# Seven block products for the second half of the output gate, with the queues around them reordered

## What is computed

```python
mod = c_act @ w_ada[l] + b_ada[l]
shift, scale, gate = jnp.split(mod, 3, axis=-1)
h = rms_norm_2(x, norm_g[l]) * (1.0 + scale[:, None, :]) + shift[:, None, :]
u = h @ w_in[l]
rg_x, rg_z, ml_x, ml_o, ml_z = jnp.split(u, split_pts, axis=-1)   # 1024 columns each
y_rg = rglru(causal_depthwise_conv(rg_x, ...), ...) * jax.nn.silu(rg_z)
y_ml = mlstm_branch(ml_x, ml_o, ...) * jax.nn.silu(ml_z)
y = jnp.concatenate([y_rg, y_ml], axis=-1) @ w_out[l]
x = x + gate[:, None, :] * y
...
# in mlstm_branch:
q = block_diag(xc, w_q); k = block_diag(xc, w_k); v = block_diag(xm, w_v)
gates = jnp.concatenate([q, k, v], axis=-1) @ w_if + b_if     # 8 columns: the "gate rows"
h = jax.nn.sigmoid(heads(o_pre)) * cell                       # o_pre is ml_o: the "output gate"
```

## Time and profile before

| | |
|---|---|
| median of 3 runs | 949.74 us (949.29 to 950.51) |
| the profiled execution's own time | 950.09 us |
| its span, first to last instruction | 948.4 us |
| TensorE busy | 877.4 us (93%) |
| DVE busy | 555.6 us (59%) |
| ACT busy | 252.9 us (27%) |
| POOL busy | 97.6 us (10%) |

### The profile page before, as it was taken

The page is one execution under the profiler, slowest core; times in us unless marked ns, Lnnn a source line. Parts: engine busy times, 40 slices in busy tenths (PEclk is TensorE's granted clock), DMA queues, the critical chain, the costliest instruction groups (busy, mean ns, idle before and its releaser), DMA issues.

```text
span 948.4 us, 14585 instructions
## 1 busy us (share of the span) xinstructions
PE 877.4 (93%) x5710; PEld 712.0 (75%) x5710; DVE 555.6 (59%) x1086; ACT 252.9 (27%) x550; POOL 97.6 (10%) x103
## 2 busy tenths in 40 slices
PE   8999999999999977766899999998999999999896
PEld 7878887888555544332789987997878898889785
DVE  4278857646222222103586893978657689667793
ACT  2356333013112110012144152032122703412311
POOL 5156000021000000001000000050000000006011
PEclk9999999999999998889899999999999999999999
DMA  9939885898999999999452633222544433522221
GB/s 342 409 140 347 363 322 209 333 422 350 367 423 420 419 420 421 421 422 384 82 208 98 223 149 119 93 86 89 187 168 168 166 134 140 216 89 90 112 88 45
DMA packets 35272, 229.58 MB, mean 242 GB/s; under 512 B 6000, under 2 KB 6032, under 8 KB 8448
## 3 DMA queue, kind: packets, MB, share of 16 engines
q1 hardware_dynamic: 31088, 222.05, 59.6%
q0 software_dynamic: 1312, 4.71, 1.4%
q10 hardware_dynamic: 2800, 1.85, 0.6%
HBM read 227.54 MB, written 1.06 MB: 241 GB/s over the span
## 4 chain that ended last, share of the span: by engine, by line
PE 69%; DVE 10%; SPq 9%; ACT 6%; DMA 3%; issue 3%; ACTq 0%; DVEq 0%
PE bank L497 12%; PE bank L994 10%; SPq L1211 8%; PE bank L1133 8%; PE bank L961 6%; PE bank L805 4%; PE bank L1035 3%; PE bank L704 3%; PE bank L1015 3%; DMA ring<-in_w_down 3%; PE bank L990 3%; PE bank L819 2%; PE bank L775 2%; PE bank L865 2%; PE bank L535 2%
## 5 line engine op out<-in xcount | busy, mean ns | idle before, releaser
L497 PE MATMUL bank<-hT,ring 128*128 128x256 f32 x512 | 113.6, 380 | 0.2 <-ACT s L1331 0.2
L497 PEld LDWEIGHTS bank<-hT,ring 128*128 128x128 f32 x512 | 96.1, 190 | 14.0 <-issue 0.8
L1921 DVE TENSOR_TENSOR x<-bank,x 128x512 f32<-128x512 f32 x32 | 22.1, 692 | 111.6 <-issue 82.7
L1133 PE MATMUL bank<-ring,s 128*128 128x256 f32 x256 | 60.0, 387 | 1.0 <-issue 1.0
L805 PE MATMUL bank<-s,z 128*32 128x256 f32 (+1 forms) x480 | 43.2, 403 | 14.5 <-DMA ws<-in_w_gate 6.5
L1133 PEld LDWEIGHTS bank<-ring,s 128*128 128x128 f32 x256 | 49.5, 194 | 8.7 <-issue 1.7
L961 PE MATMUL bank<-hT,ring 128*128 128x256 f32 x256 | 55.6, 379 | 0.0
L961 PEld LDWEIGHTS bank<-hT,ring 128*128 128x128 f32 x256 | 48.5, 190 | 6.5
L805 PEld LDWEIGHTS bank<-s,z 128*32 128x32 f32 (+1 forms) x480 | 23.3, 118 | 35.8 <-issue 24.6
L2405 POOL TENSOR_TENSOR z<-ring 128x1024 f32<-128x1024 f32 x4 | 9.4, 2352 | 387.9 <-PE bank L994 387.8
L805 PE MATMUL bank<-ring,z 128*32 128x256 f32 (+1 forms) x288 | 34.5, 409 | 6.9 <-DMA ring<-in_w_gate 4.7
(11 more groups left out here) (490 smaller groups left out, 1823.6 us busy)
## 6 DMA issues: line engine op xcount, KB each, us to landing
ring<-in_layer_pieces SPq DMA_DIRECT2D x64, 1024.0 KB, 4.9
ring<-in_first_pieces SPq DMA_DIRECT2D x49, 1024.0 KB, 7.5
s<-in_w_up SPq DMA_DIRECT2D x16, 1024.0 KB, 17.4
s<-in_w_gate SPq DMA_DIRECT2D x14, 1024.0 KB, 19.5
ring<-in_w_down SPq DMA_DIRECT2D x11, 1024.0 KB, 24.0
s<-in_w_down SPq DMA_DIRECT2D x10, 1024.0 KB, 18.6
ring<-in_w_up SPq DMA_DIRECT2D x10, 1024.0 KB, 22.0
ring<-in_w_gate SPq DMA_DIRECT2D x8, 1024.0 KB, 23.5
```

What stands on the lines that cost most here:

```text
L497: mm = pe.matmul(b[:, 0:T], w[:, (k0 + kb) * CW + m * P:(k0 + kb) * CW + (m + 1) * P], rhs[:, kb, :], start=(kb == 0), stop=(kb == nk - 1))
L1133: mm = pe.matmul(product_at(p, i), ys[r][:, kb, :], ws[w][:, kb, :], start=(kh == 0 and kb == 0), stop=(kh == 1 and kb == 3))
```

## The change

1. **mo1.** The second half of the output gate becomes a seventh pair, `mo1`, with its own `in_sums`, `pair_copy` and `in_combine`. ACT no longer takes its tanh from the bank in four parts of 256 columns; it waits until `mo1` is combined, and then takes it in two operations of 512 columns.
2. **Order on TensorE.** Two thirds of the gate rows (those of q and k) move in front of the transposes of v; then products 0 and 1 of `mo1`; then the last third; then products 2 to 6.
3. **Order on DVE.** `in_sums("mo1")` comes behind L2103, and `in_sums("mz1")` moves from behind the gate rows' chain to in front of it. The four parts of `in_combine("mo1", i)` stand before L2110, behind L2114, behind the logarithm, and behind L2125.
4. **rz0.** On ACT, `pair_copy("rz0")` moves from behind the eighth exponential and tanh pair to behind the fourth.
5. **Behind the heads.** `z_mul(1)` moves in front of the wait for the sums of squares, and the fourth difference of `weight_sums(0, 1)` behind `row_sums`.
6. **End of a layer.** The last group of products runs in the order 0, 2, 3, 4, 5, 1, 6, and `X_ORDER` is changed so that row tile 0 is complete with its sixth part and not with its seventh.
7. **End of the first block.** One multiplication by the weights moves from POOL to DVE, and one square from DVE to ACT.

The parts of the diff that carry this; semaphore counts that follow from it are left out:

```diff
-X_ORDER = ((1, 0), (0, 1), (0, 0), (1, 1), (1, 2), (0, 3), (0, 2), (1, 3))
+X_ORDER = ((1, 0), (0, 1), (0, 0), (1, 1), (0, 3), (0, 2), (1, 2), (1, 3))
+LAST_PRODUCTS = (0, 2, 3, 4, 5, 1, 6)
...
+        extra_in = {..., "mo1": late_in[1:] + [quarter(tmp[:, 1024:2048])],
...
+                pe.wait_ge(A.free, A.upto(f"mk{l}3"))
+                pe.wait_ge(S["gate_b_loaded"], 32)
+                gates = B.acquire(pe, f"gr{l}")
+                def gate_rows(lo, hi):
+                    for k in range(lo, hi, 2):
+                        for odd in range(2):
+                            src = (mqT, mkT, mvT)[k // 8]
+                            for g in range(2):
+                                q = 32 * (2 * odd + g)
+                                mm = pe.matmul(gates[q:q + MLH, 0:T], wif[:, l, k + odd, g * MLH:(g + 1) * MLH],
+                                               src[:, k % 8 + odd, :], start=(k == 0), stop=(k == 22))
+                    return mm
+                gate_rows(0, 16)
                 pe.wait_ge(A.free, A.upto(f"vn{l}11"))
                 for h in range(MLH):
                     b = A.acquire(pe, f"mv{l}{h}")
...
-                w = full(chunk())
-                out_gate_tile(2, 0, w)
+                for i in range(2):
+                    in_product("mo1", i)
                 pe.wait_ge(A.free, A.upto(f"mv{l}3"))
...
+                gate_rows(16, 24).then_inc(B.done, 1)
+                for i in range(2, 7):
+                    in_product("mo1", i)
                 for i in range(7):
                     in_product("mz0", i)
...
-                        for i in ((0, 5, 2, 3, 4, 6) if p == kh == 0 else range(7)):
+                        for i in ((0, 5, 2, 3, 4, 6) if p == kh == 0 else LAST_PRODUCTS if p == kh == 1 else range(7)):
... ACT
+                for h in range(KB):
+                    if h == KB // 2:
+                        pair_copy("rz0")
+                    step(f(aa[:, h, :], thr[:, h, :], ACT.Exp, ...))
+                    step(f(tl[:, h, :], thr[:, h, :], ACT.Tanh, ...), S["rg_gate"])
...
-                out_copy(oth[:, 0, 2 * CW:3 * CW], CW, ACT.Tanh, scale=0.5)
+                pair_copy("mo1")
                 act.wait_ge(S["lf_wanted"], l + 1)
                 step(f(rows[:, 2, :], rows[:, 2, :], ACT.Exp, scale=-1.0), S["lf_ready"])
-                out_copy(oth[:, 1, 2 * CW:3 * CW], CW, ACT.Tanh, scale=0.5)
-                out_gate(3)
                 act.wait_ge(S["row_wanted"], l + 1)
                 step(f(rows[:, 2, :], rows[:, 2, :], ACT.Exp, scale=-1.0), S["row_ready"])
+                act.wait_ge(A.free, A.upto(f"mo1{l}3"))
+                for tt in range(TT):
+                    step(f(oth[:, tt, 2 * CW:4 * CW], oth[:, tt, 2 * CW:4 * CW], ACT.Tanh, scale=0.5), S["gates_tanh"])
... DVE
+                in_sums("mo1")
                 v.wait_ge(A.free, A.upto(f"mk{l}3"))
                 in_sums("mz0")
+                in_sums("mz1")
+                in_combine("mo1", 0)
                 v.wait_ge(S["gate_b_loaded"], 32)
                 b = B.take(v)
...
-                in_sums("mz1")
-                v.wait_ge(S["gates_tanh"], TT * (l + 1))
-                v.wait_ge(A.free, A.upto(f"mo{l}31"))
+                in_combine("mo1", 3)
+                v.wait_ge(S["gates_tanh"], 2 * TT * (l + 1))
                 step(tsc(oth_t[:, :], oth_t[:, :], 1.0, None, ALU.add))
...
+                z_mul(1)
                 roots_n["ssq"] += 8
                 v.wait_ge(S["ssq_ready"], roots_n["ssq"])
                 rstd(small[:, 24:32], small[:, 16:24], 0.25 / MLD)
...
-                z_mul(1)
-                weight_sums(0, 1)
+                weight_sums(0, 1, (0, 1, 2))
... (ymT, then)
                 row_sums()
+                weight_sums(0, 1, (3,))
                 weight_sums(1, 0)
... combine(1)
+                    add_to_x(5, low)
+                    step(tten(c11, product(1), p1, ALU.add))
+                    mean_of(0)
+                    gate_it(6, c11)
+                    root_of(0)
+                    into_x(6, c11)
+                    step(tten(top, product(6), top, ALU.add))
+                    add_to_x(7, top)
                     scale_out(0)
                     mean_of(1)
                     root_of(1)
```

More of the change, by code:

```diff
@@ L333, in build @@
         late_in = [quarter(s) for s in (s7[:, 1024:2048], z1[:, 0:1024], z1[:, 1024:2048])]
-        extra_in = {"rz0": early, "rz1": late_in, "mx0": early, "mo": late_in,
+        extra_in = {"rz0": early, "rz1": late_in, "mx0": early, "mo": late_in, "mo1": late_in[1:] + [quarter(tmp[:, 1024:2048])],
                     "mz0": extra_of[0], "mz1": extra_of[1]}
@@ L392, in build @@
         chunk_of = {tag: L0 + i for i, tag in enumerate(tail)}
-        IN_KEYS = ("rz0", "rz1", "mx0", "mo", "mz0", "mz1")
+        IN_KEYS = ("rz0", "rz1", "mx0", "mo", "mo1", "mz0", "mz1")
         PAIRS_IN = {"rz0": [("in2", D), ("in2", D + CW)],
@@ L418, in pair_parts @@
         def pair_parts(key):
-            if key == "mo":
-                return oth[:, 1, 0:CW], oth[:, 1, CW:2 * CW], oth[:, 0, 0:CW], oth[:, 0, CW:2 * CW]
+            if key in ("mo", "mo1"):
+                c = 2 * CW if key == "mo1" else 0
+                return tuple(oth[:, tt, c + j * CW:c + (j + 1) * CW] for tt in (1, 0) for j in range(2))
             m = 4 * int(key[2])
@@ L431, in pair_half @@
             half = bank[:, i * CW:(i + 1) * CW]
-            return half if key == "mo" else half.rearrange("p (m t) -> p m t", m=2)
+            return half if key in ("mo", "mo1") else half.rearrange("p (m t) -> p m t", m=2)
         def product_at(p, i):
@@ L1009, in _ @@
                         projT(w, m, hT, A, f"mx{l}{2 * j + m}")
-                    used()
-                def out_gate_tile(j, tt, w):
-                    b = A.acquire(pe, f"mo{l}{j}{tt}")
-                    for kb in range(KB):
-                        mm = pe.matmul(b[:, 0:CW], hT[:, kb, tt * P:(tt + 1) * P], w[:, kb, :],
-                                       start=(kb == 0), stop=(kb == KB - 1))
-                    mm.then_inc(A.done, 1)
-                def out_gate(j):
-                    w = full(chunk())
-                    for tt in range(TT):
-                        out_gate_tile(j, tt, w)
                     used()
@@ L1544, in _ @@
                     step(f(mth[:, m, :], mc[:, m, :], ACT.Tanh, scale=0.5), S["mtanh_ready"])
-                def out_gate(j):
-                    for tt in range(TT):
-                        out_copy(oth[:, tt, j * CW:(j + 1) * CW], CW, ACT.Tanh, scale=0.5)
                 pair_copy("mo")
@@ L2160, in weight_sums @@
                     w = of_weights(full(slots_of[slot[na]]), full(slots_of[slot[nb]]), extra_of[kh])
-                    for d, s, e in (("T3", "B22", "B12"), ("T1", "B12", "B11"), ("T2", "B22", "T1"), ("T4", "B21", "T2")):
+                    differences = (("T3", "B22", "B12"), ("T1", "B12", "B11"), ("T2", "B22", "T1"), ("T4", "B21", "T2"))
+                    for i in some:
+                        d, s, e = differences[i]
                         step(tten(w[d], w[s], w[e], ALU.subtract), S["sums_ready"])
@@ L2260, in product @@
                     def product(i):
-                        v.wait_ge(S["product_done"], 14 * l + 7 * p + i + 1)
+                        at = LAST_PRODUCTS.index(i) if p else i
+                        v.wait_ge(S["product_done"], 14 * l + 7 * p + at + 1)
                         return product_at(p, i)
                     v.wait_ge(S["first_copied"], 2 * l + p + 1)
-                    step(tten(c11, product(1), p1, ALU.add))
-                    add_to_x(4 * p, c11)
+                    if p == 0:
+                        step(tten(c11, product(1), p1, ALU.add))
+                        add_to_x(0, c11)
+                        step(tten(top, product(2), p1, ALU.add))
+                        step(tten(low, product(3), top, ALU.add))
+                        step(tten(top, product(4), top, ALU.add))
+                        step(tten(last, product(4), low, ALU.add))
+                        add_to_x(1, last)
+                        step(tten(low, product(5), low, ALU.add))
+                        add_to_x(2, low)
+                        step(tten(top, product(6), top, ALU.add))
+                        add_to_x(3, top)
+                        return
                     step(tten(top, product(2), p1, ALU.add))
```

72 lines of the change are left out of this document (28 added, 44 removed).

## The result

The changed kernel takes 936.5 us (median of 4 runs, 935.39 to 938.21), the kernel before in the same job 950.12 us (949.29 to 951.87): ratio 0.9857, 95% interval 0.9839 to 0.9875. The forecast was 935.8 us. The profiled execution takes 936.42 us with a span of 934.7, so 13.7 us less span than before.

The account below looks back on a forecast made before the run. TensorE, busy 877.4 of 948.4 us, was taken as the bound. Terms 5.0 + 2.8 + 3.0 + 0.8 + 0.6 + 1.7 = 13.9 us took 950.09 to 936.2, the median 0.35 lower at 935.8; range 932.5 to 940.5.

Parts of the forecast that it names:

- Seventh pair: Second half of the output gate on TensorE: 56 instructions instead of 64, 1.73 us saved per layer.
- v's transposes: Gate rows of q and k cover TensorE's wait before the transposes of v: 0.75 us saved.
- rz0's copy: TensorE's stall before rz1 goes entirely, the copy coming behind four pairs: 1.41 us per layer, 2.8 in all.
- Behind the heads: Reordered DVE work shortens TensorE's stall in the transposes of the heads: 1.5 us per layer, 3.0 in all.
- Clock behind the heads of layer 0: With the stall cut to about 0.7, no clock fall behind the heads in either layer: 1.7 us gained.
- End of a layer: New order of last products and additions: 0.4 us per layer, 0.8 in all, bounds 0.3 and 2.0.
- DVE's time: Despite eleven more operations per layer, DVE reaches the gate rows with 0.6 us to spare; bank 3 margin 1.0.
- a wait of DVE for `ring`: Sign of being wrong: DVE waiting for `ring` ahead of the gate rows.
- End of the first block: A multiplication replaces DVE's square, so TensorE restarts 0.85 us earlier; 0.6 taken, bounds 0.4 and 0.9.
- DVE meets POOL's last difference: Rival: with a chain 1.9 us longer, z_mul(0) ends 3.2 later, losing about 2.6 per layer: 941.0; chance 0.1.
- The late piece: Rival: mz1's second piece lands at 8.8 us, TensorE loses 2.3 per layer: 940.4; chance 0.06, slower or level 0.04.

Follow-up runs that it names:

- heads_old: The changed kernel with z_mul(1) and the fourth difference of weight_sums(0, 1) put back in front of ymT; 942.16 us.
- end1_old: The changed kernel with the moves at the end of the first block undone (multiplication back on POOL, square back on DVE); 936.43 us.
- end_old: The changed kernel with the old order of a layer's last products (0 to 6) and of the last additions to x; 937.63 us.
- loads_held: The changed kernel with SP holding the first layer's weight pieces, from the third on, until DVE has the diagonal for TensorE's first transposes; 935.91 us.
- rz0_late: The changed kernel with the copy of rz0's first product put back behind the eighth exponential and tanh pair; 941.08 us.
- held_end1_old: The changed kernel with the changes of loads_held and end1_old together; 936.65 us.
- short_chain: The changed kernel with ACT copying mz0 ahead of its wait for the tanh, and the addition of 1 to the output gate split in two halves; 935.31 us.
- dve_plus: The changed kernel with two repeats of the last difference of mz1 (2.5 us more on DVE) in front of the gate rows; 940.47 us.
- mz1_late: The changed kernel with the differences of mz1 moved back behind the last combining of mo1; 953.99 us.
- both: The changed kernel with the changes of loads_held and short_chain together; 934.91 us.

## Why the prediction was right, and where it was not

The sum was 13.9 us, of which 13.3 in the second block; measured 13.7 and 14.27.

- *Seventh pair* (1.73 per layer): right, 1.73 and 1.74.
- *v's transposes* (0.75): what is left of 4.07 after 1.65 and 1.73 is 0.69, and the bracket is gone. Not tried by itself.
- *rz0's copy* (1.41): 1.65 measured. The stall went entirely, and with it 0.24 that the bracket does not contain.
- *Behind the heads* (1.5): 1.47 by `heads_old`, from 2.20 to 0.73; the forecast "under 1 us" held.
- *Clock behind the heads of layer 0* (1.7): 1.69, brought back by bringing back the stall. The fall in front of the first numerator, which I left as it is, went in layer 1 and stayed in layer 0: 0.72 more. It was not forecast and is no steady part of the change, so I count it as luck: among the seven profiles with the change's code at this place it comes in layer 0 in four (the change, `end1_old`, `end_old`, `loads_held`), in layer 1 in two (`rz0_late`, `held_end1_old`), and in neither in one (`heads_old`).
- *End of a layer* (0.4 each): 0.35 and 0.40 between the profiles. At the end of the kernel only 0.12 of the 0.40 is due to the order; no run shows what the other 0.28 is due to.
- *DVE's time*: it was to have 0.6 us to spare at the gate rows. In layer 0 it waited 0.61 for them; in layer 1 the piece came 3.62 us after DVE was free (it landed 5.9 us after its issue, 4.9 were forecast), and DVE read the gate rows 0.66 later, counted from the start of `mz0`, than in layer 0. The chain from the gate rows to the addition took 847.43 - 827.93 = 19.50, predicted 19.6. Bank 3 was empty at 845.94, and TensorE wanted it at 846.49: a margin of 0.55 where 1.0 was forecast. From the end of v to the start of `mz0` TensorE took 19.42, "about 19" was forecast. DVE was no loss against the forecast, but in layer 1 it, and not TensorE, sets the time in front of the first numerator, and 0.95 more lay there for `short_chain` to take. The 0.66 is not the reason, since `z_mul(0)` ends 1.07 behind POOL's third difference in both layers. The prediction named DVE's wait for the piece both as a sign of being right and, as "a wait of DVE for `ring`", as one of being wrong; it came in both layers (2.38 and 3.62) and put off nothing on TensorE.
- *End of the first block* (0.6): this step failed. It took for granted that TensorE restarts when DVE has the diagonal, because the bracket of before named DVE. Before it did (0.13 us behind it), but the next limit stood close. DVE was 0.65 earlier, TensorE 0.58 later in absolute time and 0.26 later by its own wait. `end1_old`, `loads_held` and `held_end1_old` show what stood behind it: with six pieces of 1 MB on the DMA engines the 16 KB packet of q8 comes late, and TensorE starts 1.63 to 1.71 us behind it. The term's mechanism was right with the loads away (0.96), and worth nothing at the projections with them.

So the stretch up to the projections came out 1.17 worse than in the sum (0.57 lost instead of 0.6 gained; 0.31 of that arose earlier in the first block, which the change does not touch), and the second block 0.97 better, mostly by the clock of layer 1 (0.72) and `rz0` (0.48 in two layers). The two cancel by chance: the total is nearer than its parts.

Of the rivals, "DVE meets POOL's last difference" did not happen (`z_mul(0)` took 2.13 in layer 1, 3.00 in layer 0, each behind POOL's third), nor did it in any run. Its room, forecast at 1.9, was 1.13 in layer 1 and 2.00 in layer 0. With a chain 2.5 us longer (`dve_plus`) POOL's start moved too, `z_mul(0)` met the third again, and the loss was 1.31 and 2.89. With 5 us more (`mz1_late`) the meeting came elsewhere and was dearer than the 2.6 per layer of the rival: not one blocked instruction, but two on DVE and two on POOL, and the lower clock behind the wait, 8.8 and 9.4 per layer with the work itself. L2134 has one input and waited as long as the differences with two. It moves 2048 columns in the 1.23 us that a difference needs for 1024. The Trainium skill ("SBUF — State Buffer", Who interferes with whom) counts a tensor_scalar in a two-port mode among the instructions that exclude GpSimd's, the later one waiting for the whole of the other; the trace agrees in both directions, with 3.25 against 1.23 and 3.20 against 2.36. My rival had used the half of that rule on two SBUF inputs only, and so looked at `z_mul(0)` alone. The late piece did occur in part: it cost DVE 0.66 at the gate rows of layer 1, and the margin at bank 3, 1.21 in layer 0, was 0.55 there. TensorE lost nothing by it.

## What to carry to other kernels

A stall's price is its bracket, what the products beside it lose and the lower clock that may follow: here 1.41 was worth 1.65, and 1.47 with its fall 3.2. When work is moved to where an engine "had time", find what that engine will meet if it comes late: the same four differences were free in front of the gate rows and cost 9 us per layer behind them, in layer 1 2.9 as work, 4.0 as blocking and 2.45 at the lower clock. And an idle bracket that names an engine tells who came last in that execution, not who comes next: before pricing a faster predecessor, look at what else reaches its end at the same moment, the DMA engines among it.

## What the hardware showed that I had not expected

- *TensorE's restart behind loads.* Between the blocks TensorE starts 1.63 to 1.71 us behind a packet of 16 KB of the queue q8, kind "instruction", unless DVE is later. With the DMA engines full (share about 1.0) that packet starts 3.3 to 4.2 us after TensorE's last matmul, with the loads held 0.93. In the whole of the changed kernel q8 moves 47 such packets, 0.77 MB. The Trainium skill ("Advanced Engine Details and Errata", ISA Cache) gives the instruction cache lines of 16 KB, and the packets agree. That the packet holds TensorE's next instructions is argued from this; the trace does not say whose they are.
- *DVE and POOL in turns.* Two instructions of each that overlap cost both engines: 4.0 us on DVE and 1.7 on POOL, and with the work itself and the lower clock behind TensorE's wait 9 us of time per layer (`mz1_late`). A single meeting costs DVE the rest of POOL's instruction: in eight measured cases of before, the change, `dve_plus` and `short_chain` `z_mul(0)` ended 1.07 to 1.09 us behind the difference of POOL that it met.
- *The clock.* A fall kept TensorE at 1.2 instead of 2.4 GHz for 3.4 us in most places, 6.8 behind the first block (10.2 in `heads_old`), 4.2 to 7.1 at the end of the kernel and 13.7 in each layer of `mz1_late`. What one costs depends on who sets the time there: in front of the first numerator 1.66 with the short DVE chain (22.71 against 21.05 in the same layer, `short_chain` and `both`), and 0.73 where DVE was the limit (22.72 against 21.99 in `rz0_late`). Behind the heads it came in three of the four cases with a stall of 2.19 to 2.35 (not in layer 1 of before), and in none of 22 with 0.73. Why the one in front of the first numerator comes in one layer or execution and not in another stays open: `short_chain` and `both` have the same code there.
